# One plain up panel instead of two at the head of each MLP, in a two-layer hybrid transformer with a third mixer on Trainium2

## What is computed

```python
def sq_relu_mlp(h, w_up, w_down):
    return jnp.square(jax.nn.relu(h @ w_up)) @ w_down      # w_up 1024 x 4096, w_down 4096 x 1024

for layer in range(2):
    ...
    h = h + mixer(rms_norm(h, g_mix[layer]), ...)
    h = h + sq_relu_mlp(rms_norm(h, g_mlp[layer]), w_mlp_up[layer], w_mlp_down[layer])
```

## Time and profile before

| | before |
|---|---|
| median of 3 runs | 1629.88 us (1629.73 to 1630.76) |
| profiled execution | 1630.15 us, span 1628.4 us |
| PE busy | 1598.7 us, 98% |
| VectorE busy | 1016.4 us, 62% |
| ScalarE busy | 725.8 us, 45% |
| GpSimd busy | 271.0 us, 17% |
| granted TensorE clock | 0.998 of full speed, mean |
| PE in the chain that ended last | 91% of the span |

### The profile page before, as it was taken

How to read it: one execution, slowest core, us unless ns; L and a number is a source line. 1 busy time by engine, 2 the same in 40 slices (tenths; PEclk the granted TensorE clock), 3 DMA queues, 4 the chain that set the end, 5 groups by cost and what they waited for, 6 DMA issues and landing times.

```text
span 1628.4 us, 29172 instructions
## 1 busy us (share of the span) xinstructions
PE 1598.7 (98%) x12203; PEld 1417.2 (87%) x12203; DVE 1016.4 (62%) x1416; ACT 725.8 (45%) x1144; POOL 271.0 (17%) x222
## 2 busy tenths in 40 slices
PE   8999999999999999999999999999999999989998
PEld 7998677899999999999887898888887788667896
DVE  6534666388666666555557867677756547856544
ACT  5533554465444444331235544444445445675323
POOL 1002212132222222110004222222212000000200
PEclk9999999999999999999999999999999999999999
DMA  6231030123332222232232333222256676001001
GB/s 197 78 78 31 22 84 10 54 78 130 104 104 89 94 84 99 84 99 93 88 104 78 130 104 104 96 90 100 97 103 99 118 96 89 19 1 62 28 28 52
DMA packets 122689, 134.29 MB, mean 82 GB/s; under 512 B 18877, under 2 KB 99508, under 8 KB 122564
## 3 DMA queue, kind: packets, MB, share of 16 engines
q1 hardware_dynamic: 122362, 132.44, 29.7%
q10 hardware_dynamic: 202, 0.06, 0.0%
HBM read 126.13 MB, written 2.10 MB: 79 GB/s over the span
## 4 chain that ended last, share of the span: by engine, by line
PE 91%; DVE 4%; ACT 2%; issue 1%; DMA 1%; SPq 1%; ACTq 0%; DVEq 0%
PE ps L483 30%; PE ps L1703 22%; PE ps L1650 17%; PE ps L2699 2%; PE ps L829 2%; PE ps L1674 2%; PE ps L812 2%; PE ps L939 1%; PE ps L1220 1%; PE ps L2427 1%; PE ps L837 1%; PE ps L3224 1%; PE ps L2871 1%; PE ps L2850 1%; PE ps L2866 1%
## 5 line engine op out<-in xcount | busy, mean ns | idle before, releaser
L453 ACT ACTIVATE w_hi<-raw 128x1024 fp32r<-128x1024 f32 (+2 forms) x171 | 179.4, 1051 | 400.4 <-PE ps L483 249.4
L483 PE MATMUL ps<-x_hi,w_hi 128*128 128x512 f32 (+4 forms) x872 | 245.8, 333 | 0.5 <-DVE x_lo L503 0.4
L483 PE MATMUL ps<-x_lo,w_hi 128*128 128x512 f32 (+4 forms) x872 | 239.7, 326 | 0.0
L483 PE MATMUL ps<-x_hi,w_lo 128*128 128x512 f32 (+4 forms) x872 | 239.1, 325 | 0.0
L460 DVE TENSOR_TENSOR w_lo<-raw,w_hi 128x1024 fp32r<-128x1024 f32 (+2 forms) x171 | 206.5, 1222 | 45.1 <-ACT w_hi L453 45.1
L1703 PE MATMUL ps<-a_hi,w_hi 128*128 128x258 f32 (+1 forms) x768 | 204.2, 320 | 0.3 <-DVE h L1887 0.3
L1703 PE MATMUL ps<-a_hi,w_lo 128*128 128x258 f32 (+1 forms) x768 | 204.1, 320 | 0.0
L1703 PE MATMUL ps<-a_lo,w_hi 128*128 128x258 f32 (+1 forms) x768 | 204.0, 320 | 0.0
L483 PEld LDWEIGHTS ps<-x_hi,w_hi 128*128 128x128 f32 (+2 forms) x872 | 145.4, 187 | 19.2 <-issue 3.1
L483 PEld LDWEIGHTS ps<-x_lo,w_hi 128*128 128x128 f32 (+2 forms) x872 | 144.6, 186 | 16.4 <-issue 2.2
L483 PEld LDWEIGHTS ps<-x_hi,w_lo 128*128 128x128 f32 (+2 forms) x872 | 144.6, 187 | 14.7
(11 more groups left out here) (489 smaller groups left out, 3343.2 us busy)
## 6 DMA issues: line engine op xcount, KB each, us to landing
raw<-in_w_mlp_up SPq DMA_DIRECT2D x32, 1024.0 KB, 5.3
raw<-in_w_mlp_down SPq DMA_DIRECT2D x32, 1024.0 KB, 5.0
raw<-in_w_in SPq DMA_DIRECT2D x16, 1024.0 KB, 9.6
raw<-in_w_in_conv SPq DMA_DIRECT2D x12, 1024.0 KB, 5.0
raw<-in_w_in_attn SPq DMA_DIRECT2D x8, 1024.0 KB, 5.2
raw<-in_w_out_attn SPq DMA_DIRECT2D x4, 1024.0 KB, 5.0
raw<-in_w_out_conv SPq DMA_DIRECT2D x4, 1024.0 KB, 4.9
raw<-in_w_out SPq DMA_DIRECT2D x4, 1024.0 KB, 5.8
```

The costliest lines, as they stand in the source:

```text
L453: act.activation(split_tile(w_hi, t), raw_tile(t), ACT.Copy).then_inc(w_hi_ok, 1)
L483: ins = pe.matmul(tile_banks(t)[0:m, b, 0:c], w[:, k, :], x[:, k, x0:x0 + c], start=(k == order[0] and n == 0), stop=(k == order[-1] and n ...
```

## The change

Up panel 1 becomes a panel of seven products, so that only panel 0 is plain (`PLAIN = 1`). Up panel 2, also of seven products, follows it without a down panel between. Since panel 0's banks are still in use, panel 1's sums stand in banks 6 and 7 (`P_BANK_FIRST`), in which the norm's statistics were.

In all panels of products the order changes to 1, 7, 6, 2, 5, 4, 3, and more is summed in PSUM: products 1, 6, 5 and 3 in one bank, a copy of product 1 and product 2 in a second, 7 and 4 in a third. The copy of product 1 goes to PSUM instead of SBUF. The temporaries `s1` and `s75` and their additions go, and two of the four quarters get relu and scale straight out of PSUM. The chunk with tile 1 is squared ahead of the one with tile 0.

The queues of ScalarE and VectorE are written anew for panels 0 to 2: weight parts and copies of panel 1 stand ahead of the squares of panel 0. The mixing of the activations starts two tiles sooner in the projection before the MLP. GpSimd makes the sums for panel 1 too.

The diff, cut to its core (the queue of VectorE in the projection changes as ScalarE's does):

```diff
-        ORDER = (1, 5, 7, 2, 6, 3, 4)
+        ORDER = (1, 7, 6, 2, 5, 4, 3)
         X_ROW = {5: 0, 6: 1, 7: 2, 4: 3}
-        P_BANK = {1: 0, 6: 0, 2: 1, 7: 2, 4: 2, 5: 3, 3: 3}
+        P_BANK = {1: 0, 6: 0, 5: 0, 3: 0, 2: 1, 7: 2, 4: 2}
+        P_BANK_FIRST = {1: 6, 6: 6, 5: 6, 3: 6, 2: 7, 7: 2, 4: 2}
         W_AT = {4: 8, 5: 12, 7: 16, 6: 20, 3: 24}
         PART_READERS = ((1, 2), (4,), (5, 7), (6, 3))
-        PLAIN = 2
+        PLAIN = 1
...
+        def fast_bank(u, m):
+            return (P_BANK_FIRST if u == PLAIN else P_BANK)[m]
...
-                if j in (4, 6):
-                    mix_hi(act, nxt, j // 2 - 2)
-                if j in (3, 5):
-                    mix_made(act, nxt, j // 2 - 1)
+                if j in (2, 4, 6):
+                    mix_hi(act, nxt, j // 2 - 1)
+                if j % 2:
+                    mix_made(act, nxt, j // 2)
...
             if m == 1:
                 pe.wait_ge(w_lo_ok, t + 1)
                 if first:
-                    pe.wait_ge(evicted, MLP_T0[layer] + 2)
+                    pe.wait_ge(scale_ok, nm.n + 1)
+                elif u == PLAIN + 1:
+                    pe.wait_ge(evicted, up_tile(layer, u - 1) + 1)
                 else:
-                    pe.wait_ge(copied, 3 * n)
-            if m == 5:
+                    pe.wait_ge(evicted, up_tile(layer, u - 1) + 2)
+            if m == 7:
                 pe.wait_ge(p_lo, 2 * n + 1)
                 if first:
+                    pe.wait_ge(evicted, MLP_T0[layer] + 1)
                     pe.wait_ge(xs["lo"], 4 * layer + 4)
                 else:
-                    pe.wait_ge(added, 3 * n)
-            if m == 7 and not first:
-                pe.wait_ge(evicted, up_tile(layer, u - 1) + 2)
-            if m == 2 and not first:
-                pe.wait_ge(evicted, up_tile(layer, u - 1) + 1)
+                    pe.wait_ge(added, 2 * n)
             if m == 6:
                 pe.wait_ge(copied, 3 * n + 1)
                 pe.wait_ge(p_lo, 2 * n + 2)
-            if m == 3:
-                pe.wait_ge(added, 3 * n + 1)
+            if m == 5:
+                pe.wait_ge(copied, 3 * n + 3)
             if m == 4:
                 pe.wait_ge(w_lo_ok, t + 2)
                 pe.wait_ge(copied, 3 * n + 2)
+            if m == 3:
+                pe.wait_ge(added, 2 * n + 1)
...
+            m, dst = ((1, ps[:, fast_bank(u, 2), :]), (7, s7), (6, s6))[which]
             act.wait_ge(product, product_at(layer, u, m))
             if u > PLAIN:
-                before = up_tile(layer, u - 1)
                 if which == 0:
-                    act.wait_ge(evicted, before + 1)
-                if which == 1:
-                    act.wait_ge(added, 3 * n - 2)
-                if which == 2:
-                    act.wait_ge(evicted, before + 2)
-            act.activation(dst[:, 0:hw], ps[:, P_BANK[m], 0:hw], ACT.Copy).then_inc(copied, 1)
+                    act.wait_ge(evicted, up_tile(layer, u - 1) + 1)
+                else:
+                    act.wait_ge(added, 2 * n - 2 + which)
+            act.activation(dst[:, 0:hw], ps[:, fast_bank(u, m), 0:hw], ACT.Copy).then_inc(copied, 1)
 
         def square_act(act, nm, layer, u, tile):
...
+            elif tile:
+                act.wait_ge(scaled, nth_up(layer, u) + 1)
             else:
-                act.wait_ge(scaled, 2 * nth_up(layer, u) + tile + 1)
+                act.wait_ge(evicted, up_tile(layer, u) + 2)
...
         def up_act(act, nm, layer, u):
-            t = up_tile(layer, u)
             if u == 0:
-                mix_made(act, nm, 2)
-                mix_hi(act, nm, 2)
-                split_hi(act, t + 2)
+                mix_hi(act, nm, 3)
+                prep_act(act, layer, 1, 0)
+                prep_act(act, layer, 1, 2)
                 norm_scale(act, nm)
+                prep_act(act, layer, 1, 3)
+                copy_act(act, nm, layer, 1, 0)
+                prep_act(act, layer, 1, 1)
+                copy_act(act, nm, layer, 1, 1)
                 square_act(act, nm, layer, 0, 0)
-                mix_made(act, nm, 3)
-                split_hi(act, t + 3)
-                mix_hi(act, nm, 3)
+                copy_act(act, nm, layer, 1, 2)
                 square_act(act, nm, layer, 0, 1)
             elif u == 1:
                 prep_act(act, layer, 2, 0)
                 prep_act(act, layer, 2, 2)
+                prep_act(act, layer, 2, 3)
+                copy_act(act, nm, layer, 2, 0)
+                square_act(act, nm, layer, 1, 1)
+                prep_act(act, layer, 2, 1)
                 square_act(act, nm, layer, 1, 0)
-                prep_act(act, layer, 2, 3)
-                prep_act(act, layer, 2, 1)
-                square_act(act, nm, layer, 1, 1)
             else:
                 t = mlp_tile(MLP_T0[layer], "down", u - 2)
-                for y in range(2):
-                    split_hi(act, t + y, free=t + y - 3)
-                copy_act(act, nm, layer, u, 0)
+                if u > PLAIN + 1:
+                    split_hi(act, t, free=t - 3)
+                    split_hi(act, t + 1, free=t - 2)
+                if u > PLAIN + 1:
+                    copy_act(act, nm, layer, u, 0)
                 copy_act(act, nm, layer, u, 1)
                 copy_act(act, nm, layer, u, 2)
+                if u == PLAIN + 1:
+                    split_hi(act, t, free=t - 3)
+                    split_hi(act, t + 1, free=t - 2)
+                square_act(act, nm, layer, u, 1)
                 square_act(act, nm, layer, u, 0)
-                square_act(act, nm, layer, u, 1)
...
+            n, hw, f = nth_up(layer, u), nm.width // 2, nm.first
+            b0, b1, b2 = [ps[:, fast_bank(u, m), 0:hw] for m in (1, 2, 7)]
+            read = FF // P * layer + 2 * u
             if what == "11":
                 dve.wait_ge(product, product_at(layer, u, 2))
+                dve.wait_ge(a_lo_ok, read)
+                dve.scalar_tensor_tensor(tmp[:, 0, hw:2 * hw], b1, 0.0, scale_bc[:, f + hw:f + 2 * hw], ALU.max, ALU.mult).then_inc(evicted, 1)
             if what == "22":
+                dve.wait_ge(copied, 3 * n + 2)
+                dve.wait_ge(product, product_at(layer, u, 5))
+                dve.tensor_tensor(tmp[:, 1, 0:hw], s7[:, 0:hw], b0, ALU.add).then_inc(added, 1)
+            if what == "21":
                 dve.wait_ge(copied, 3 * n + 3)
+                dve.wait_ge(product, product_at(layer, u, 4))
+                dve.tensor_tensor(tmp[:, 1, hw:2 * hw], s6[:, 0:hw], b2, ALU.add).then_inc(added, 1)
             if what == "12":
                 dve.wait_ge(product, product_at(layer, u, 3))
+                dve.scalar_tensor_tensor(tmp[:, 0, 0:hw], b0, 0.0, scale_bc[:, f:f + hw], ALU.max, ALU.mult).then_inc(evicted, 1)
+
+        def scale_dve(dve, nm, layer, u):
+
+            n, w = nth_up(layer, u), nm.width
+            dve.wait_ge(added, 2 * n + 2)
+            dve.scalar_tensor_tensor(tmp[:, 1, 0:w], tmp[:, 1, 0:w], 0.0, scale_bc[:, nm.first:], ALU.min, ALU.mult).then_inc(scaled, 1)
...
             if u == 0:
-                t = up_tile(layer, 0)
-                mix_dve(dve, nm, 2)
-                mix_lo(dve, nm, 2)
+                mix_lo(dve, nm, 3)
+                prep_dve(dve, layer, 1, 0)
+                prep_dve(dve, layer, 1, 2)
                 dve.wait_ge(scale_ok, nm.n + 1)
                 plain_take(dve, nm, layer, 0, 0)
-                split_lo(dve, t + 2)
+                prep_dve(dve, layer, 1, 3)
+                plain_take(dve, nm, layer, 0, 1)
+                prep_dve(dve, layer, 1, 1)
                 a_low(dve, nm, layer, 0, 0)
-                mix_dve(dve, nm, 3)
-                plain_take(dve, nm, layer, 0, 1)
-                split_lo(dve, t + 3)
-                mix_lo(dve, nm, 3)
                 a_low(dve, nm, layer, 0, 1)
             elif u == 1:
+                add("11")
                 prep_dve(dve, layer, 2, 0)
-                plain_take(dve, nm, layer, 1, 0)
+                add("22")
                 prep_dve(dve, layer, 2, 2)
+                add("21")
+                add("12")
+                prep_dve(dve, layer, 2, 3)
+                scale_dve(dve, nm, layer, 1)
+                a_low(dve, nm, layer, 1, 1)
                 a_low(dve, nm, layer, 1, 0)
-                prep_dve(dve, layer, 2, 3)
-                plain_take(dve, nm, layer, 1, 1)
                 prep_dve(dve, layer, 2, 1)
-                a_low(dve, nm, layer, 1, 1)
             else:
                 t = mlp_tile(MLP_T0[layer], "down", u - 2)
                 split_lo(dve, t)
                 split_lo(dve, t + 1)
-                add("75")
                 add("11")
                 add("22")
+                add("21")
+                scale_dve(dve, nm, layer, u)
                 add("12")
-                scale_dve(dve, nm, layer, u, 0)
-                add("21")
-                scale_dve(dve, nm, layer, u, 1)
```

(7 more changed lines are left out.)

54 lines of the change are left out of this document (18 added, 36 removed).

## The result

The changed kernel takes a median of 1635.79 us (1634.46 to 1639.52, 7 runs), the kernel before 1630.47 us beside it (1627.61 to 1632.43, 7 runs). The ratio is 1.0039, with a 95% interval of 1.0028 to 1.0049: 0.39% slower. The forecast was 1635.2.

The account below looks back on a forecast made before the run. TensorE, busy in 98% of the span, was taken as the bound. Savings and four added waits summed to +2.8 us in the first MLP and +2.5 in the second, together +5.3: median 1635.2 us, range 1630.0 to 1638.5.

Parts of the forecast that it names:

- four places: Late waits forecast in each MLP: scale before panel 1, product 3 of panel 1, products 5 and 3 of panel 2.
- The saving: Up panel 1 as seven products: 1.73 us less in the first MLP, 2.00 in the second, 0.4 in its down panel 0.
- The scale: Panel 1's first product waits for ScalarE's exponential, mixing being held by GpSimd's sums: 1.05 us late, second MLP 1.4.
- S: Start of up panel 1, forecast at 361.08 instead of 360.02 in the first MLP.
- The three waits in the products: Addition "22" of panel 1 1.15 us late; in panel 2, copy of product 6 1.1 and addition "22" 1.2.
- S2: Start of up panel 2, forecast at 372.35 in the first MLP.
- the two waits of panel 2: Product 5 waits for the copy of 6, 1.1 us; product 3 for "22" behind the down splits, 1.2 us.
- GpSimd not holding the mixing: Rival at panel 1's start: mixing steps keep their turn, the scale is in time; median 1630.8, up to 1632; chance 0.2.
- ScalarE in time for panel 2: Faster rival: ScalarE reaches panel 2's copies in time; with the mixing unheld, -4.1 us, median 1625.8; chance 0.08.
- The late load: Slower rival: up panel 3's load lands late, costing 1 to 2 us in each MLP; 1637 to 1639; chance 0.12.
- The new order itself free in the steady panels: Claim for panel 3 onward: no idle, least slack 0.8 us, panels of 10.05 and 9.95 us.
- the whole possible gain: Both MLPs with every wait met in time, including down panel 0's idle: -4.1 us, 0.25%.

Follow-up runs that it names:

- e8: Changed kernel reordered on four engines in panels 0 to 2 and down panel 0, with GpSimd's first two panel 1 sums made early; 1625.93 us, ratio 0.9988.
- e1: Changed kernel with one wait more: GpSimd starts panel 1's sums only after VectorE's last mixing step; 1636.48 us, ratio 1.0035.
- e4: Changed kernel with panel 2's copies of products 7 and 6 sooner on ScalarE, part 1's low part sooner on VectorE; 1636.32 us, ratio 1.0044.
- e7: New order of products alone, with two plain panels as in the kernel before; 1640.86 us, ratio 1.0058 to the kernel before.
- e3: Changed kernel with addition "22" of panel 1 ahead of the low part of panel 2's weight part 0 on VectorE; 1632.93 us, ratio 1.0009.
- e5: Changed kernel with additions "11" and "22" of panel 2 ahead of the two down splits in VectorE's queue; 1638.64 us, ratio 1.0047.
- e2: Changed kernel with ScalarE's weight parts 0 and 2 of panel 1 ahead of the last high part of the mixing; 1636.14 us, ratio 1.0038.

## Why the prediction was right

The mechanism was right in its four places; how close the number came is partly luck. The forecast had +5.3 us, and the medians differ by 5.32. But the two heads lost 6.18 us, and the ratio of 1.0039 is 6.4: the sum was some 0.9 us short, as shown below.

**The saving.** I took 1.73 and 2.00 us for the panel and 0.4 for down 0 of the second MLP. The first MLP's head in e8 bears it out: 1.61 less, with 0.11 lost in up 0. The second has 1.59 less: -2.00, another 0.52 from down 0, and two losses, 0.46 in up 0 (12.47 against 12.01), which e8's early sums bring, and 0.47 in the products.

**The scale.** Foretold: sums at about 352, three mixing steps of 1.4, S late by 1.05 and 1.4 us. Measured: sums at 350.22 in a head that starts 1.9 us sooner, steps of 1.42, 1.42 and 1.39; S at 13.41 us behind up 0, where before it was 12.40 (1.01 late), and in the second MLP at 13.40, before 12.01 (1.39 late). e1 shows the cause.

**The three waits in the products.** Foretold 1.15, 1.1 and 1.2 us. From the start of the matmul ahead of each wait to the start behind it, less the usual 0.12, the first MLP lost 1.23, 1.08 and 1.03 us, the second 1.28, 1.15 and 1.02. The sum of the three, 3.34 and 3.45, is what I had (3.45 and 3.5). The places and the order of the queues are those of the prediction: the copies of panel 2 ran from 376.82, which is 6.1 us behind S2 (370.7), as worked out. What the list of prices hides is that the two waits of panel 2 can't be won one by one: by e4 they are one chain with two gates. Take the first away and the second takes its time.

**Mis-sized: the restart.** This is the term that the sum lacks. Behind each wait the first matmul takes 0.36 to 0.39 us, and the next starts 0.19 to 0.23 behind it, not 0.12. Four waits cost 0.38 us more in each MLP. With them, and 0.07 at product 6 of panel 1, the first MLP comes to -1.73 + 1.01 + 3.34 + 0.38 + 0.07 = +3.07, measured +3.06, foretold +2.8.

**Mis-sized: the second MLP.** -2.00 + 1.39 + 3.45 + 0.38 - 0.52 makes +2.7; measured is +3.12, foretold +2.5. Another 0.32 us lies in small steps that no wait view lists: 0.07 in panel 1, and 0.18 and 0.07 at product 6 of panel 2. e8 has the same step at product 6 (0.17 us), without any wait around it. I read the panel's 9.95 us as what two panels in a row would take each, and in the second MLP they take a little more. The trace shows what product 6 meets there: VectorE's low part of part 3 ends at 908.92, and product 6 starts at 909.07, right behind it; in the first MLP it has 0.3 us to spare. It is late because ScalarE starts the high part 0.54 us behind the start of panel 2 instead of 0.26. Why it does so in the second MLP alone is open, and so is the last 0.1 us.

**The rivals.** GpSimd not holding the mixing fell by the first three rows of the mixing and by e1. ScalarE in time for panel 2 fell with the copies at S2+6.1. The late load fell: no wait in panel 3 or down 0. The new order itself free in the steady panels: held, e7.

**Not foreseen at all:** that the missing gain was to be had. I called -4.1 us the whole possible gain and gave it 0.08, by ScalarE happening to be in time; e8 gets 3.2 of it by orders alone.

## What to carry to other kernels

When a wait is taken away, ask which step has the next least slack, since TensorE arrives there sooner by just what was won: of five single edits one won its whole wait (e3), one gained half a microsecond to a microsecond in each head (e5), one nothing (e2), and two lost (e1; e4 by the clock). A run of GpSimd operations belongs where VectorE is idle or works out of PSUM, and sums of a panel that has landed early can be made in such a gap; this one move was worth 2.3 us of 9.4. A new order of steps is to be judged by its steady panels and its entry apart: here it was free in 26 panels and cost up to 3.7 us in a head, through the first one.
